# Second output-projection halves ahead of the router transposes, fewer warm-up matmuls, one set of expert weights asked ahead of another

## The chip, the cores and the metric

The kernel runs on one core of a Trainium2 chip. The metric is device time in microseconds (us) for one execution. Five compute engines run their own instruction lists and meet at semaphores: TensorE (PE, matmuls into PSUM banks), VectorE (DVE), ScalarE (ACT), GpSimd (POOL) and SyncE (SP, which here only issues DMAs). Weight loads of TensorE are listed apart as PEld.

## The reference

One layer for 128 context tokens and 512 latent tokens, five tiles of 128 tokens, with a model width of 1024. Cut to what matters here:

```python
x = x + g1 * m                                    # m: mixer output, [y_conv, y_ret] @ w_out
xn = rmsnorm(x, norm_ffn_g) * (1 + sc2) + sh2
x = x + g2 * hier_moe(xn, ...)

# hier_moe
lg_group = t @ w_rg + b_rg                        # 4 groups
gidx = argmax(lg_group)
lg_in = (t @ w_re + b_re) of group gidx           # 8 experts in the group
topv, topi = top_k(lg_in, 2)
w_sel = softmax(topv) * softmax(lg_group)[gidx]
acc = sum over the 2 chosen experts of w_sel * ((silu(t @ w1) * (t @ w3)) @ w2)
```

There are 32 experts of width 256; each has 3 MB of float32 weights: gate (w1), up (w3) and down (w2), 1 MB each. After the layer comes a last norm.

## The kernel before, in words

The order of the work is written out by hand, one instruction list for each engine. The stages: modulation and input projection, convolution and retention, the output projection with the router, and the experts.

**The output projection and the router.** `project(t, half)` multiplies tile t by one half (512 columns) of the output weights, 24 matmuls for tiles 1 to 4 (lines 1138 to 1140, three products of high and low parts for each of eight row blocks), and counts in `wout_mm`. For each half, VectorE's `residual` adds the result to x (`x1_ready`). After both halves `second_norm` writes the tile's normed rows (line 1855, `xn2_ready`), with the sum of squares and the root from ScalarE. `router_T(t)` (line 1359) waits for these rows and transposes them in eight matmuls; ScalarE copies them out of PSUM in two halves (line 1039, `xn2T_ev`); `router(t)` (line 1370) multiplies the copies by the router weights, its first half waiting for the first copy. VectorE's `choose(t)` picks the experts; `ranks(t)` on TensorE (lines 1380 and 1381) counts the tokens before each one; VectorE's `place(t)` writes the slot of each token, and `slots(t)` (line 1390) gathers the slots. For tile t the loop on TensorE runs the projection of tile t beside the router of tile t-1; only for t = 1 do both projection halves come before the transposes.

**From the last tile to the first expert.** On TensorE: `slots`, `ranks(3)`, `clock(14)`, the transposes of tile 4, `clock(2)`, its router, `picked_rows(3)`, `clock_on(5)`, `ranks(4)`, `gathered_rows`, `picked_rows(4)`, `slots(4)`. `clock` and `clock_on` multiply the identity by itself into a bank that is not read (lines 1423 and 1428). `picked_rows` and `gathered_rows` (line 1433) build the rows of the first two experts; the gathered part comes from a DMA that GpSimd issues at line 741 (`first_rows_in`).

**The experts.** Each expert has 64 slots. `gate_up` runs 16 matmuls of 256 columns (lines 1488 and 1492), then VectorE and ScalarE form the hidden values, and `down` (line 1508) multiplies them out.

**The weights of the experts.** Six sets of buffers: `e_slot = (1, 2, 0, 4, 3, 5)`. Some are laid over memory that the output projection uses. `released(sp, slot, FIRST_EXPERT_ITEM)` waits for nine projection halves for slots 0 and 1 (the last tile's first half) and for ten for slots 2 and 3. So set 0 (slot 1) and set 2 (slot 0) are free one projection half before set 1 (slot 2). From the seventh expert on SyncE waits for the gate and up products of the expert that held the slot (`gu_mm`, line 623).

Of the kernel before, what the change touches and what calls it, by code (L numbers as in the profile page):

```python
# [35 lines left out]
FIRST_EXPERT_ITEM = ADA_ALL + N_IN + 2  # L36
# [96 lines left out]
def layer(nc, a, y_prompt, y_sample, new_f, new_b):  # L133
# [8 lines left out]
    with ExitStack() as ctx:  # L142
# [227 lines left out]
        def proj_groups(n):  # L370

            return CB * min(n, 3) + NT * max(n - 3, 0)
# [23 lines left out]
        e_slot = E_SLOTS  # L396
# [59 lines left out]
        def w_down(s, c):  # L456

            if s == RING and c == 0:
                return expert_slot(s)[:, 0:D]
            if s == RING + 1 and c == 1:  # L460
                return arena_b[:, 4352:4352 + D]
            return expert_slot(s)[:, 2 * KT * DE + D * c:2 * KT * DE + D * c + D]
# [20 lines left out]
        def released(eng, slot, item):  # L483

            before = [n for n in range(item) if SLOTS[n] == slot]
            if not before:
                return
            kind, s = items[before[-1]]
            if item == FIRST_EXPERT_ITEM:
                eng.wait_ge(wout_mm, 2 * NT - 1 + (slot in (2, 3)))  # L490
            elif slot == 3 and len(before) == 1:

                eng.wait_ge(proj_mm, proj_groups(N_IN))
            elif kind == "ada":
                eng.wait_ge(mod_mm, s + 1)
            elif kind == "in":

                eng.wait_ge(w_lo_ready, 4 * (s + 1) + 3)
            else:
                eng.wait_ge(wout_mm, 2 * NT - 1 + s)  # L500
# [5 lines left out]
        def _(sp):  # L506
# [11 lines left out]
            def gate_up_weights(s, gate_src, up_src):  # L518
                sp.dma_start(w_gate(s), gate_src).then_inc(ring_in[s], 16)  # L519
                sp.dma_start(w_up(s), up_src).then_inc(ring_in[s], 16)  # L520
# [39 lines left out]
            def gate_up_of(n):  # L560
                gate_up_weights(e_slot[n % NSLOT], gv[n], uv[n])
# [9 lines left out]
            def residual_rows_out(t):  # L571
                sp.wait_ge(x1_ready, 2 * t + 2)
                sp.dma_start(x1_rows[P * t:P * t + P, :], x[:, t, :]).then_inc(x1_out[t // 2], 16)
# [5 lines left out]
            def normed_rows_away(tiles):  # L579
                sp.wait_ge(xs_out[tiles[0] // 2], 16 * len(tiles))  # L580
                sp.wait_ge(xn2T_mm, 2 * tiles[-1] + 2)
# [7 lines left out]
            def down_part_of(n, c):  # L589
                sp.dma_start(w_down(e_slot[n], c), dv[n][:, c, :]).then_inc(down_in[e_slot[n]], 16)  # L590
# [12 lines left out]
            up_of(5)  # L603
            normed_rows_away((2, 3))
            down_part_of(3, 0)
            released(sp, e_slot[1], FIRST_EXPERT_ITEM)
            gate_up_of(1)
            residual_rows_out(NT - 1)
            released(sp, e_slot[2], FIRST_EXPERT_ITEM)
            gate_up_of(2)  # L610

            residual_rows_away((NT - 1,))
            down_part_of(3, 1)
# [476 lines left out]
        def _(pe):  # L1090
# [184 lines left out]
            def late_mod_row(n):  # L1275

                pe.wait_ge(mod_ev, LATE_MODS[n] + 1)
                if n == 0:
                    pe.wait_ge(modrow_ev, len(ROW_MODS))
                    pe.wait_ge(mod_ev, LATE_MODS[0])  # L1280
                    pe.wait_ge(b_late_in, 16 * 2)
                pe.matmul(bank[7 - n][96:98, :], k("sel_rows")[0:SUM_ROWS + 1, 0:2], late_sum[n][0:SUM_ROWS + 1, :],
                          start=True, stop=True).then_inc(modrow_mm, 1)
# [43 lines left out]
            def project(t, half, steps=range(KT)):  # L1327
                n = 2 * t + half
                if t == 0:
                    landed(pe, ADA_ALL + N_IN + half)  # L1330
                if n >= 4 and steps[0] == 0:
                    pe.wait_ge(x1_ready, n - 3)
                if n == 2:
                    pe.wait_ge(mod_ev, ADA_ALL)
                if t == 1:
                    pe.wait_ge(high_act, out_high_done(half, 3))
                    pe.wait_ge(low_dve, (3, 5)[half])
                    pe.wait_ge(low_pool, out_low_done(half))
                if t >= 1 and half == 0:
                    pe.wait_ge(high_act, y_high_done(t, 1))  # L1340
                    pe.wait_ge(low_pool, y_low_done(t))
                w = wide(ADA_ALL + N_IN + half)
                for kt in steps:
                    if t >= 1:
                        low = y_part(t, kt // CB)[1][:, kt % CB, :]
                        last = split_product(bank[n % 4][:, :], (y_hi[(t - 1) % 2][:, kt, :], low),
                                             (out_hi[half][:, kt, :], out_lo[half][:, kt, :]), kt == 0, kt == KT - 1)
                        continue
                    lhs = yconvT[:, kt, P * t:P * t + P] if kt < CB else yretT[:, t, kt - CB, :]
                    last = pe.matmul(bank[n % 4][:, :], lhs, w[:, kt, :], start=(kt == 0), stop=(kt == KT - 1))  # L1350
                if steps[-1] == KT - 1:
                    last.then_inc(wout_mm, 1)

            def router_T(t):
                pe.wait_ge(xn2_ready, t + 1)
                for kt in range(KT):
                    if t >= 1 and kt % 4 == 0:
                        pe.wait_ge(xn2T_ev, 2 * t - 1 + kt // 4)
                    last = pe.transpose(bank[4 + kt // 4][:, P * (kt % 4):P * (kt % 4) + P], xn2[t][:, kt:D:KT], ident)
                    if kt % 4 == 3:  # L1360
                        last.then_inc(xn2T_mm, 1)

            def router(t):
                pe.wait_ge(xn2T_ev, 2 * t + 1)
                if t >= 1:
                    pe.wait_ge(lg_ready, t)
                for kt in range(KT):
                    if kt == HALF_K:
                        pe.wait_ge(xn2T_ev, 2 * t + 2)
                    last = pe.matmul(bank[6][:, 0:GROUPS + EXPERTS], xn2T[:, t % 2, kt, :], w_router[:, kt, :],  # L1370
                                     start=(kt == 0), stop=(kt == KT - 1))
                last.then_inc(rt_mm, 1)

            def ranks(t):

                pe.wait_ge(chosen, t + 1)
                if t >= 1:
                    pe.wait_ge(placed, t)
                both = rt[:, BOTH + EXPERTS * (t % 2):BOTH + EXPERTS * (t % 2) + EXPERTS]
                pe.matmul(bank[7][:, 0:32], k("before"), both, start=True, stop=True)  # L1380
                pe.matmul(bank[7][:, 32:64], k("ones").broadcast_to([P, P]), both, start=True, stop=True).then_inc(rank_mm, 1)
# [13 lines left out]
            for t in range(NT):  # L1395
                project(t, 0)
                if t == 0:
                    late_mod_row(0)
                    late_mod_row(1)
                if t == 1:  # L1400
                    project(t, 1)
                if t >= 1:
                    router_T(t - 1)

                if t == NT - 1:
                    router(t - 1)
                if t == NT - 1:
                    project(t, 1, range(HALF_K + 1))
                    ranks(t - 2)
                    project(t, 1, range(HALF_K + 1, KT))  # L1410
                elif t != 1:
                    project(t, 1)
                if 1 <= t < NT - 1:
                    router(t - 1)
                if t == 3:
                    slots(t - 3)
                if 2 <= t < NT - 1:
                    ranks(t - 2)
            def clock(turns):

                pe.wait_ge(x1_ready, 2 * NT)
                for _ in range(turns):
                    pe.matmul(bank[0][:, 0:P], ident, ident, start=True, stop=True)

            def clock_on(turns):

                for _ in range(turns):
                    pe.matmul(bank[3][:, 0:P], ident, ident, start=True, stop=True)
# [9 lines left out]
            def picked_rows(t):  # L1438

                pe.wait_ge(x1_ready, 2 * NT)  # L1440
                pe.wait_ge(picked, t - NT + 3)
                first_pair(xn2[t], pick[t], t == NT - 2, t == NT - 1)
# [7 lines left out]
            slots(NT - 4)  # L1450
            slots(NT - 3)
            ranks(NT - 2)
            clock(14)
            router_T(NT - 1)
            clock(2)
            router(NT - 1)
            slots(NT - 2)
            picked_rows(NT - 2)
            clock_on(5)
            ranks(NT - 1)  # L1460
            gathered_rows()
            picked_rows(NT - 1)
# [767 lines left out]
```

## Time and profile before

| | us |
|---|---|
| median of 3 runs | 668.73 |
| lowest, highest | 667.97, 671.67 |
| the profiled execution | 670.74 |
| its span, first to last instruction | 669.1 |
| its mean granted TensorE clock | 0.968 |

The page gives the busy share of each engine over the whole span: TensorE 92%, VectorE 48%, GpSimd 24%, ScalarE 23%. These are means over stages with different limits. In the slices of the page the DMA engines are full from about 418 us on, and mostly not full in the stages before; TensorE is full in most slices until about 470 us. Matmul ends are modelled, so that the step from one start to the next says more than the duration of one. A wait for several semaphores is put down to the last of them.

### The profile page before, as it was taken

The numbers are of one execution on the slowest core, as the hardware profiler recorded it, in microseconds if no ns is written. First come the engines' busy times: TensorE is split into PE (matmuls) and PEld (weight loads), VectorE is DVE, ScalarE is ACT, GpSimd is POOL, SyncE is SP. The second block draws the span as 40 slices with busy tenths as digits, with TensorE's granted clock in tenths as the row PEclk, the third lists the DMA queues.
The fourth block names the chain that finished last, engine by engine and source line by source line (L and its number), as shares of the span: only waits on it lengthen the run. The fifth ranks groups of instructions, "written<-read, shape, count | busy, mean of one in ns | idle before, by whom it ended". The sixth has DMA issues, their size and how long they took to land.

```text
span 669.1 us, 9054 instructions
## 1 busy us (share of the span) xinstructions
PE 612.7 (92%) x3712; PEld 437.3 (65%) x3712; DVE 318.4 (48%) x631; ACT 154.1 (23%) x297; POOL 160.4 (24%) x124
## 2 busy tenths in 40 slices
PE   3799999999999989999699899999998788889796
PEld 3579999988888865744588797555554444445342
DVE  1433118706240445718768763455454555334326
ACT  5325432122312233354221111101101000001014
POOL 0042724333242200027330011222221111111110
PEclk9989999999999999999799889999999888899999
DMA  7985240320303269788552798999999999999977
GB/s 278 387 295 219 70 153 1 126 89 37 126 0 126 69 227 394 255 317 323 190 196 89 292 390 331 414 418 418 420 417 417 418 420 417 421 417 418 416 279 299
DMA packets 50381, 183.83 MB, mean 275 GB/s; under 512 B 5861, under 2 KB 6037, under 8 KB 38945
## 3 DMA queue, kind: packets, MB, share of 16 engines
q1 hardware_dynamic: 42156, 161.59, 61.9%
q0 software_dynamic: 7216, 18.99, 7.9%
q10 hardware_dynamic: 964, 2.63, 1.1%
q8 instruction: 31, 0.51, 0.3%
q14 instruction: 14, 0.11, 0.0%
HBM read 172.79 MB, written 16.81 MB: 283 GB/s over the span
## 4 chain that ended last, share of the span: by engine, by line
PE 66%; DMA 20%; DVE 7%; SPq 4%; ACT 2%; issue 1%; DVEq 0%; POOLq 0%; ACTq 0%
PE bank L1138 12%; PE bank L1139 11%; PE bank L1140 11%; PE bank L1488 9%; DMA ring<-in_w_up_e 8%; DMA arena_ab<-in_w_up_e 4%; DMA x<-in_w_up_e 4%; PE bank L1508 4%; PE bank L1097 3%; DMA ring<-expert_out_rows 2%; PE bank L1433 2%; PE bank L1114 2%; DVE out_lo L480 1%; SPq L519 1%; PE bank L1192 1%
## 5 line engine op out<-in xcount | busy, mean ns | idle before, releaser
L1488 PE MATMUL bank<-ring,arena_ab 128*64 128x256 f32 x352 | 83.3, 392 | 10.1 <-DMA ring<-in_w_up_e 9.6
L680 POOL TENSOR_TENSOR w_lo<-ring,w_hi 128x1024 fp32r<-128x1024 f32 x25 | 61.4, 2458 | 112.5 <-ACT w_hi L864 112.5
L1492 PE MATMUL bank<-ring,arena_ab 128*64 128x256 f32 x352 | 83.3, 392 | 0.0
L1488 PEld LDWEIGHTS bank<-ring,arena_ab 128*64 128x64 f32 x352 | 48.9, 141 | 46.8 <-DMA ring<-in_w_up_e 17.5
L1622 DVE TENSOR_TENSOR arena_ab<-arena_ab,bank 64x256 f32<-64x256 f32 x32 | 19.5, 610 | 113.3 <-ACT arena_ab L1045 113.3
L1138 PE MATMUL bank<-arena_ab_r,w_hi 128*128 128x320 f32 x192 | 62.2, 324 | 3.0 <-DVE xn_lo L1622 2.9
L786 POOL DMA_INDIRECT expert_out_rows<-arena_ab,row_out x32 | 32.0, 1001 | 130.9 <-DVE arena_ab L1622 130.9
L1138 PE MATMUL bank<-w_hi,arena_ab_r 128*128 128x512 f32 x160 | 63.3, 396 | 0.0
L1139 PE MATMUL bank<-w_lo,arena_ab_r 128*128 128x512 f32 x160 | 62.9, 393 | 0.0
L1140 PE MATMUL bank<-w_hi,xn_lo 128*128 128x512 f32 x160 | 62.8, 393 | 0.0
L1139 PE MATMUL bank<-xn_lo,w_hi 128*128 128x320 f32 x192 | 59.9, 312 | 0.0
L1140 PE MATMUL bank<-arena_ab_r,w_lo 128*128 128x320 f32 x192 | 59.8, 311 | 0.0
L1045 ACT ACTIVATE arena_ab<-bank 64x256 f32<-64x256 f32 x32 | 12.0, 376 | 205.0 <-PE bank L1492 205.0
L864 ACT ACTIVATE w_hi<-ring 128x1024 fp32r<-128x1024 f32 x25 | 26.5, 1062 | 114.1 <-PE bank L1140 114.1
L1492 PEld LDWEIGHTS bank<-ring,arena_ab 128*64 128x64 f32 x352 | 48.9, 141 | 0.0
L1508 PE MATMUL bank<-ring,arena_ab 128*64 128x512 f32 x176 | 42.6, 605 | 0.9 <-ACT arena_ab L1049 0.9
L1138 PEld LDWEIGHTS bank<-arena_ab_r,w_hi 128*128 128x128 f32 x192 | 36.9, 192 | 6.1 <-issue 5.0
L1140 PEld LDWEIGHTS bank<-arena_ab_r,w_lo 128*128 128x128 f32 x192 | 37.0, 193 | 0.0
L1139 PEld LDWEIGHTS bank<-xn_lo,w_hi 128*128 128x128 f32 x192 | 37.0, 193 | 0.0
L1140 PEld LDWEIGHTS bank<-w_hi,xn_lo 128*128 128x128 f32 x160 | 30.0, 188 | 7.2
L1139 PEld LDWEIGHTS bank<-w_lo,arena_ab_r 128*128 128x128 f32 x160 | 30.1, 188 | 6.7
L1138 PEld LDWEIGHTS bank<-w_hi,arena_ab_r 128*128 128x128 f32 x160 | 30.1, 188 | 6.6
(289 smaller groups left out, 1123.1 us busy)
## 6 DMA issues: line engine op xcount, KB each, us to landing
ring<-in_w_ada SPq DMA_DIRECT2D x11, 2048.0 KB, 12.3
ring<-in_w_down_e SPq DMA_DIRECT2D x22, 1024.0 KB, 25.8
ring<-in_w_gate_e SPq DMA_DIRECT2D x22, 1024.0 KB, 23.1
ring<-in_w_up_e SPq DMA_DIRECT2D x22, 1024.0 KB, 26.0
ring<-in_w_in SPq DMA_DIRECT2D x6, 2048.0 KB, 8.4
arena_ab<-in_w_down_e SPq DMA_DIRECT2D x15, 512.0 KB, 24.0
x<-in_w_gate_e SPq DMA_DIRECT2D x5, 1024.0 KB, 25.8
arena_ab<-in_w_gate_e SPq DMA_DIRECT2D x5, 1024.0 KB, 24.0
```

Source lines behind the costliest of these rows:

```text
L680: pool.tensor_tensor(as_piece(w_lo[p_ % 2], p_), piece_of(w, p_), as_piece(w_hi[p_ % 2], p_), ALU.subtract).then_inc(w_lo_ready, 1)
L786: pool.indirect_dma_start(half_rows, bass.IndirectOffsetOnAxis(ap=column, axis=0), ysb[:, p_, :], None, bounds_check=2 * 2 * TOK - 1, oob_ ...
L864: act.activation(as_piece(w_hi[piece % 2], piece), piece_of(w, piece), ACT.Copy).then_inc(w_hi_ready, 1)
L1097: last = pe.matmul(out[32 * j:32 * j + 32, :], cs[:, kt, :], w[:, kt, :], start=(kt < 4), stop=(kt >= 4))
L1114: last = pe.matmul(bank[4 + 2 * (t % 2) + half][:, P * c:P * c + P], x[:, t, P * kt:P * kt + P], diag[:, t, :], start=True, stop=True)
L1138: pe.matmul(out, lhs[0], rhs[0], start=start, stop=False)
L1139: pe.matmul(out, lhs[0], rhs[1], start=False, stop=False)
L1140: return pe.matmul(out, lhs[1], rhs[0], start=False, stop=stop)
L1488: pe.matmul(bank[2 + p_][0:BLK, 0:DE], lhs, w_gate(s)[:, kt, :], start=(kt == 0), stop=(kt == KT - 1))
L1492: last = pe.matmul(bank[2 + p_][BLK:2 * BLK, 0:DE], lhs, w_up(s)[:, kt, :], start=(kt == 0), stop=(kt == KT - 1))
L1508: last = pe.matmul(bank[6 + p_][BLK * half:BLK * half + BLK, :], hidT[:, p_, c, :], w_down(s, c)[:, SL * half:SL * half + SL], start=(c == ...
L1622: return dve.tensor_tensor(out, in0, in1, op)
```

## The change

Three edits, all of order or count. On TensorE, the second projection halves of tiles 2 and 3 come before the transposes of the tile in front, as that of tile 1 does already. The warm-up matmuls after `ranks(3)` are 5 and not 14, those before `ranks(4)` 2 and not 5. On SyncE, the gate and up weights of set 2 are asked for before those of set 1, and the residual rows of the last tile are sent out after both.

```diff
@@ SyncE
             down_part_of(3, 0)
+            released(sp, e_slot[2], FIRST_EXPERT_ITEM)
+            gate_up_of(2)
             released(sp, e_slot[1], FIRST_EXPERT_ITEM)
             gate_up_of(1)
             residual_rows_out(NT - 1)
-            released(sp, e_slot[2], FIRST_EXPERT_ITEM)
-            gate_up_of(2)
@@ TensorE
-                if t == 1:
+                if t in (1, 2, 3):
                     project(t, 1)
                 if t >= 1:
                     router_T(t - 1)
...
-                elif t != 1:
+                elif t not in (1, 2, 3):
                     project(t, 1)
                 if 1 <= t < NT - 1:
                     router(t - 1)
...
             ranks(NT - 2)
-            clock(14)
+            clock(5)
             router_T(NT - 1)
...
             picked_rows(NT - 2)
-            clock_on(5)
+            clock_on(2)
             ranks(NT - 1)
```

On TensorE, in the turn of tile 2, this is the place between the two projection halves (the high and low parts of the first half's weights are out_hi_53 and out_lo_55, those of the second half out_hi_54 and out_lo_56; line 1359 is the transposes of tile 1):

```order
 L1139 MATMUL bank<-out_lo_55,arena_cd_r 128x512
 L1140 MATMUL bank<-out_hi_53,arena_ab_r 128x512
-L1359 MATMUL bank<-kept,arena_ab 128x128 x8
 L1138 MATMUL bank<-out_hi_54,arena_cd_r 128x512
 L1139 MATMUL bank<-out_lo_56,arena_cd_r 128x512
```

The eight transposes leave this place, and the two halves follow each other. On TensorE, 24 matmuls later in the same turn, this is the end of the second half (line 1370 is the router of tile 1, line 1380 the ranks of tile 0):

```order
 L1139 MATMUL bank<-out_lo_56,arena_cd_r 128x512
 L1140 MATMUL bank<-out_hi_54,arena_ab_r 128x512
+L1359 MATMUL bank<-kept,arena_ab 128x128 x8
 L1370 MATMUL bank<-w_router,arena_ab 128x36 x8
 L1380 MATMUL bank<-arena_cd,kept 128x32
```

Transposes and router of one tile now stand side by side; the turn of tile 3 reads the same. On SyncE, after the last projection's first half, the requests stand like this (line 519 asks for gate weights, line 520 for up weights, line 573 sends residual rows out):

```order
 L519 DMA ring<-in_w_gate_e 128x2048
 L520 DMA ring<-in_w_up_e 128x2048
-L573 DMA residual_rows<-x 128x1024
 L519 DMA ring<-in_w_gate_e 128x2048
 L520 DMA ring<-in_w_up_e 128x2048
+L573 DMA residual_rows<-x 128x1024
 L590 DMA arena_ab<-in_w_down_e 128x1024
```

The residual rows move behind both pairs; which set a pair belongs to does not show in the rows, but the first pair is now set 2 and the second set 1. The lists of VectorE, ScalarE and GpSimd are the same in both kernels.

## Rows read from the trace of the kernel before

**Rows 1.** Windows: us, busy by engine, PEclk, DMA share, GB/s.

```profile
380.00:382.00 2.00, 1.06 (x5) 0.53 (x3) 1.89 (x8) 0.00 (x0) 0.88 (x1) 1.00 0.14 57
406.00:408.00 2.00, 1.56 (x21) 1.24 (x21) 1.45 (x7) 1.81 (x2) 0.19 (x1) 1.00 0.59 119
480.00:630.00 150.00, 129.11 (x876) 69.04 (x874) 70.76 (x125) 12.42 (x38) 26.57 (x28) 0.94 1.02 418
```

**Rows 2.** Timeline of SyncE: start, us, line, operation; the requests for weights.

```profile
369.78 0.33 SPq L519 DMA_DIRECT2D ring<-in_w_gate_e  x1
...
381.09 0.33 SPq L519 DMA_DIRECT2D ring<-in_w_gate_e  x1
...
383.25 0.45 SPq L519 DMA_DIRECT2D ring<-in_w_gate_e  x1
...
394.78 0.33 SPq L519 DMA_DIRECT2D ring<-in_w_gate_e  x1
...
410.37 0.33 SPq L519 DMA_DIRECT2D ring<-in_w_gate_e  x1
```

**Rows 3.** Chain that ended last, from 383 us: start, us, what.

```profile
383.37 4.83 PE bank L1423 x28
...
395.83 2.00 PE bank L1428 x10
...
398.19 7.71 PE bank L1433 x32
...
406.67 0.40 PE bank L1488
```

**Rows 4.** Timeline of TensorE, tile 3's transposes and router [idle before <-releaser].

```profile
369.59 1.04 PE L1359 MATMUL bank<-kept,arena_ab 128*128 128x128 f32 x8
371.45 1.95 PE L1370 MATMUL bank<-w_router,arena_ab 128*128 128x36 f32 x16 [0.83 <-ACT arena_ab L1039]
```

**Rows 5.** Timeline of VectorE, last tile's residual, normed rows and choice.

```profile
369.78 0.69 DVE L1622 TENSOR_TENSOR arena_cd<-bank,arena_ab 128x512 f32<-128x512 f32 x1 [1.71 <-PE bank L1140]
...
384.90 1.28 DVE L1855 SCALAR_TENSOR_TENSOR arena_ab<-arena_ab,stat 128x1024 f32<-128x1024 f32 x1
...
394.72 0.92 DVE L1622 TENSOR_TENSOR arena_cd<-arena_cd 128x8 f32<-128x8 f32 x5
```

**Rows 6.** Timeline of TensorE, transposes and routers of tiles 0 and 1.

```profile
331.67 1.04 PE L1359 MATMUL bank<-kept,arena_ab 128*128 128x128 f32 x8
332.96 1.97 PE L1370 MATMUL bank<-w_router,arena_ab 128*128 128x36 f32 x16 [0.25 <-ACT arena_ab L1039]
334.77 0.48 PE L1138 MATMUL bank<-out_hi,arena_cd_r 128*128 128x512 f32 x1
...
340.46 1.06 PE L1359 MATMUL bank<-kept,arena_ab 128*128 128x128 f32 x8
341.28 0.48 PE L1138 MATMUL bank<-out_hi,arena_cd_r 128*128 128x512 f32 x1
...
346.97 1.87 PE L1370 MATMUL bank<-w_router,arena_ab 128*128 128x36 f32 x16
348.68 0.39 PE L1380 MATMUL bank<-arena_cd,kept 128*128 128x32 f32 x2
```

**Rows 7.** Timeline of GpSimd, the first gather's issue.

```profile
385.73 1.41 POOL L741 DMA_INDIRECT arena_cd<-expert_in_rows,idx  x1 [3.66 <-DVE idx L1841]
```

**Rows 8.** DMA issues over the span: count, KB, median us to landing.

```profile
ring<-in_w_up_e SPq DMA_DIRECT2D x22, 1024.0 KB, 26.0
...
arena_cd<-expert_in_rows,idx POOLq DMA_INDIRECT x16, 8.5
```

**Rows 9.** Windows around the routers of tiles 0 and 3, PEclk third from the end.

```profile
332.70:336.11 3.41, 3.16 (x23) 2.92 (x23) 2.08 (x4) 2.97 (x7) 2.11 (x2) 1.00 0.38 154
...
370.24:373.66 3.42, 2.59 (x22) 2.39 (x21) 3.00 (x15) 1.08 (x2) 0.00 (x0) 1.00 0.86 275
373.66:377.07 3.41, 3.41 (x10) 2.66 (x9) 2.89 (x18) 0.00 (x0) 0.00 (x0) 0.50 1.02 428
```

## The prediction

> **What bounds the kernel now.** I read the windows first, stage by stage, since the average over the span hides that there are two limits. From 480 to 630 us the DMA engines are full at 418 GB/s and TensorE waits inside the expert loop [rows 1]: there the load stream is the bound. Before that, around 380 us, the lanes moved 57 GB/s, and at 406 to 408 us 119 GB/s [rows 1], so they had room. The second view is SyncE's own issue list. After the first six sets of weights are asked for, nothing more can be asked until the first expert's gate and up products free a slot: that issue stands at 410.37 us [rows 2], 3.7 us after the first expert's first matmul at 406.67 us [rows 3]. So the full stream that ends the kernel hangs on the start of the first expert, and what moves that start moves the end by as much. What moves only a load that lands before its use moves nothing.
>
> What sets 406.67 us is the third view, the chain of waits from 363 us on. It runs on TensorE through the last projection's first half (its end is the router transpose's start, 369.59 us [rows 4]), crosses to VectorE at 369.78 us, where that engine had idled 1.71 us for the bank [rows 5], and stays with VectorE until the normed rows of the last tile are written at 384.90 + 1.28 = 386.18 us [rows 5]. Then it is TensorE's again: warm-up matmuls until 388.20 us, router, picked rows, warm-up, ranks, gathered rows at 398.19 us, first expert [rows 3].
>
> **The change, part by part.**
>
> *Second halves ahead of the router transposes, tiles 2 and 3.* No instruction is added or taken away. Before, the transposes of tile 1 took 340.46 to 341.28 us = 0.82 us, and the router matmuls, a projection half later, 346.97 to 348.68 us = 1.71 us, with no wait at either: 2.53 us [rows 6]. The half product between them covered ScalarE's copy of the transposed rows. After the change the router follows the transposes at once, as it does for tile 0 already. There the pair took 331.67 to 334.77 us = 3.10 us, with an idle of 0.25 us put down to ScalarE [rows 6]. So each of the two places costs 3.10 - 2.53 = 0.57 us, and nothing covers it, since TensorE is the engine that VectorE waits for at 369.78 us. Bounds: 0.25 us each by the idle alone, 0.83 us each by the largest such idle, at 371.45 us [rows 6, 4]; I take 0.57, the whole pair measured. What is won is that each second half ends 0.82 us sooner, so that VectorE gets its second residual and norm sooner; but VectorE already idles before 369.78 us, so this is worth nothing. ScalarE's high part of tile 4 now waits behind the copy of tile 1 and not the other way round; only the last projection uses it, a whole tile later, so it costs nothing. Sum of this part: +1.1 us on the whole chain from 369.78 us.
>
> *Warm-up 14 to 5.* The fourteen took 4.83 us, 0.345 us each, and ended at 388.20 us [rows 3], 2.0 us after the rows that the next transposes wait for. With 0.1 us for the hand-over, 1.9 us of them were too long. Five take 1.7 us, from 383.37 + 1.1 = 384.5 to 386.2 us, and the rows come at 386.18 + 1.1 = 387.3 us. So the wait for the rows takes the place of the matmuls, and the part gives back 1.9 us; TensorE idles 1.1 us instead.
>
> *Warm-up 5 to 2.* Five took 2.00 us [rows 3], 0.40 us each. VectorE's choice, for which the ranks wait behind them, was ready at 394.72 + 0.92 = 395.64 us [rows 5], when these matmuls began (395.83 us). All five are on the path, three fewer give back 1.2 us. Were each as short as half of that, as at the clock's upper level, 0.6 us.
>
> *Third set asked ahead of the second.* The slot of the third set is free one projection half sooner, so its two requests move from 383.25 us to just after the group that begins at 369.78 us; the second set's keep their place at about 381.09 us [rows 2], and the last residual rows go out behind both. 2 MB at 418 GB/s are 5.0 us of the lanes, of which part falls into the empty stretch at 380 us. The second set is asked for 25 us before the first expert even begins, the third is used after the second; both land long before. Residual rows, the remaining down parts and the fifth set follow a few us later, all used after 410 us. Worth nothing at the end by itself.
>
> The gather of the first rows could be touched: it is issued at 385.73 us and SyncE is released by it at 394.78 us, 9.05 us later [rows 2, 7]. Moved by +1.1 us it lands at 395.9 us, and the gathered rows would begin at 398.19 - 2.0 = 396.2 us: covered, with 0.3 us to spare. What it would cost if the deeper queue held it back: bounds nothing and the whole 5.0 us of the third set's transfer. I take nothing, since in the full stream such gathers land in 8.5 us while the weights asked on SyncE's queue take 26.0 us [rows 8], so a gather does not stand behind them.
> The Trainium skill, DMA: Bandwidth & Descriptors, section on queues, rings and completion order, says that each DMA engine goes round the queues that have work, packet by packet; by that rule the depth of the other queue adds nothing, which is the value taken, and the landings of the full stream agree with it [rows 8].
>
> Sum: +1.1 - 1.9 - 1.2 = -2.0 us at the first expert, and as much at the end. The profiled execution took 670.74 us (a span of 669.1 and 1.6 around it), so 668.7 us; against the median of the runs shown, 668.73 us, it is 666.7 us.
>
> **The rivals.**
>
> *The router stretches pull the clock down.* From 369.59 to 371.45 + 1.95 = 373.40 us TensorE did only transposes and router, with 0.83 us idle; the granted clock was 1.0 in 370.24 to 373.66 us and 0.50, which is 1.2 of 2.4 GHz, in the 3.41 us after [rows 4, 9]. The projection in that stretch ran at half speed: 3.41/2 = 1.7 us lost. There it cost nothing, as VectorE was late anyway. The change makes two more such stretches, of 3.1 us and the ranks behind, on the path. Against it: around the same pair of tile 0 the granted clock stayed at 1.00 from 332.70 to 336.11 us [rows 9]. It decides from both places on: -2.0 + 3.4 = +1.4 us, slower, 670.1 us. With one place it is -0.3 us, 668.4 us.
> The Trainium skill, TensorE: Matmul & The Clock Gate, section on HAM oscillation, puts the fall down to idle gaps longer than any of these. By the page the sum stays -2.0 us; the row at 373.66 us shows a fall behind 0.83 us of idle, and the measurement decides, so the rival keeps its chance.
>
> *Less warm-up, and the first expert starts at half speed.* The same rows bear it out in kind: little work, then 0.50. The gathered and picked rows lie between (7.71 us [rows 3]), which speaks against. A half-speed stretch of 3.41 us in the first expert costs 1.7 us and so holds its slot that much longer: -0.3 us, 668.4 us.
>
> *The gather comes late.* 1 us late gives -1.3 us, 667.4 us; all 5.0 us behind the new transfer gives 400.9 instead of 396.2 us, +2.7 us, 671.4 us.
>
> *The lanes are the bound already from 370 us.* Then filling the empty stretch, up to 1.7 us of 380 to 382 us, comes on top: -3.7 us, 665.0 us. Against it stand the 119 GB/s at 406 us.
>
> *The warm-up is not what the path waits for:* the rows come later than I think, only +1.1 - 1.2 remains, 668.6 us.
>
> **How the numbers follow.** Forecast, 666.7 us: 0.45. Clock after the router stretches: 0.16, a quarter of it with both places. Clock at the first expert: 0.18. Late gather: 0.10. Lanes as the bound: 0.06. Warm-up not on the path: 0.05. The order's bounds (0.5 to 1.7 us for both places) and the second warm-up's (0.6 to 1.2) make the forecast's own range 666.1 to 667.9 us. The runs shown go from 667.97 to 671.67 us, so I put about 1.5 us on either side of the cases: 664.6 to 670.4 us. Half a per cent is 3.3 us, about what can be told from no change. Below 665.4 us lie most of the lanes' case and a tail of the forecast, 0.12; above 672.1 us only the worst gather and the worst clock with a bad run, 0.03; 0.85 between.
>
> **What would show it.** Right: a router start some 0.5 us behind the transposes' end for tiles 1 and 2; the last projection's first half ending about 1.1 us later; an idle of about 1 us before the last tile's transposes, put down to VectorE, and these starting 0.8 us sooner; gathered rows and first expert 2.0 us sooner; the step from first expert to end unchanged. Wrong: a clock of 0.50 in the projection of tiles 3 or 4 or in the first expert; gathered rows that wait for a DMA; a first slot release at 408.4 us without an earlier end.

## The result and the profile after

The changed kernel takes 672.76 us (median of 20 runs, 670.20 to 675.93), the kernel before 669.46 us (median of 20 runs measured with it): a ratio of 1.0046, 95% interval 1.0034 to 1.0057, which is +3.1 us (2.3 to 3.8). The forecast was 666.7 us, within 664.6 to 670.4 us. It was wrong in sign and outside its range. The profiled execution of the changed kernel took 673.58 us, its span is 671.9 us (669.1 before), its mean granted clock 0.964.

All work up to the first router is the same code, yet that router starts at 331.57 us here and at 332.96 us in the profile before. Tile 1's second half, just ahead of that router, ran at 0.50 until 326.4 us here and until 329.3 us before. So I count every stage from the first router's start; the table gives the distance and what each stage adds. "Last" means of tile 4.

| stage begins, us behind the first router | before | after | added in the stage before it |
|---|---|---|---|
| tile 3's transposes | 36.62 | 39.25 | +2.63 |
| last transposes | 55.08 | 55.68 | -2.03 |
| picked rows (line 1433) | 58.67 | 62.24 | +2.97 |
| last ranks | 64.70 | 66.80 | -1.47 |
| first expert | 73.71 | 75.81 | 0.00 |
| last expert's last down product | 305.25 | 307.75 | +0.40 |
| end of the span | 336.15 | 340.37 | +1.72 |

The five stages to the first expert add 2.10 us, all 4.22 us; less the 1.39 us by which the first router came sooner, this is the 2.8 us between the spans.

TensorE's timeline of the changed kernel (start us, us, line, operation, [idle before <-releaser]):

```profile
344.67 1.05 PE L1359 MATMUL bank<-kept,arena_ab 128*128 128x128 f32 x8
345.96 1.98 PE L1370 MATMUL bank<-w_router,arena_ab 128*128 128x36 f32 x16 [0.24 <-ACT arena_ab L1039]
...
359.52 1.05 PE L1359 MATMUL bank<-kept,arena_ab 128*128 128x128 f32 x8
360.87 1.98 PE L1370 MATMUL bank<-w_router,arena_ab 128*128 128x36 f32 x16 [0.30 <-ACT arena_ab L1039]
...
370.82 1.04 PE L1359 MATMUL bank<-kept,arena_ab 128*128 128x128 f32 x8
372.69 1.95 PE L1370 MATMUL bank<-w_router,arena_ab 128*128 128x36 f32 x16 [0.83 <-ACT arena_ab L1039]
...
382.60 0.65 PE L1390 MATMUL bank<-b_ada_rows,modsum 128*64 128x16 f32 x16 [1.83 <-DVE b_ada_rows L1926]
...
383.92 2.10 PE L1423 MATMUL bank<-kept 128*128 128x128 f32 x10
387.25 1.97 PE L1359 MATMUL bank<-kept,arena_ab 128*128 128x128 f32 x8 [1.23 <-DVE arena_ab L1855]
389.02 1.06 PE L1423 MATMUL bank<-kept 128*128 128x128 f32 x4
389.87 3.46 PE L1370 MATMUL bank<-w_router,arena_ab 128*128 128x36 f32 x16
...
393.81 4.19 PE L1433 MATMUL bank<-arena_ab 128*128 128x128 f32 x16
397.80 0.73 PE L1428 MATMUL bank<-kept 128*128 128x128 f32 x4
...
398.73 4.05 PE L1433 MATMUL bank<-kept,arena_cd 128*128 128x128 f32 x16
...
407.38 0.40 PE L1488 MATMUL bank<-ring,arena_ab 128*64 128x256 f32 x1 [0.44 <-ACT arena_ab L1056]
```

The routers of tiles 1 and 2 now follow their transposes with the idle for ScalarE's copy, 0.24 and 0.30 us, that tile 0 had [rows 6]. Before the last transposes TensorE idles 1.23 us for VectorE's normed rows, as the forecast said. What it did not say stands in the next rows: eight transposes take 1.97 us and the router 3.46 us. In the kernel before:

```profile
382.16 0.65 PE L1390 MATMUL bank<-b_ada_rows,modsum 128*64 128x16 f32 x16 [1.10 <-DVE b_ada_rows L1926]
...
388.04 1.05 PE L1359 MATMUL bank<-kept,arena_ab 128*128 128x128 f32 x8
...
389.39 1.97 PE L1370 MATMUL bank<-w_router,arena_ab 128*128 128x36 f32 x16
...
391.63 4.19 PE L1433 MATMUL bank<-arena_ab 128*128 128x128 f32 x16
```

The transposes and the router, the same instructions, took 1.05 and 1.97 us there. The picked rows take 4.19 us in both. The gather of the slots (line 1390) is taken up under the order below. The windows of the changed kernel say why (us, busy by engine, PEclk third from the end, DMA share, GB/s):

```profile
380.00:382.00 2.00, 0.77 (x4) 0.29 (x2) 1.76 (x11) 0.00 (x0) 0.95 (x1) 1.00 1.03 328
406.00:408.00 2.00, 1.56 (x17) 1.29 (x18) 0.94 (x6) 1.34 (x2) 0.00 (x0) 1.00 0.74 262
480.00:630.00 150.00, 128.56 (x872) 68.64 (x870) 69.91 (x125) 12.39 (x38) 27.18 (x27) 0.94 1.02 418
363.92:367.33 3.41, 3.41 (x10) 2.63 (x9) 2.19 (x11) 0.00 (x0) 0.55 (x1) 0.50 0.37 154
384.40:387.81 3.41, 2.18 (x12) 1.89 (x11) 3.20 (x11) 0.85 (x3) 1.06 (x1) 0.50 1.01 425
387.81:391.22 3.41, 3.41 (x18) 3.41 (x17) 1.81 (x10) 2.48 (x3) 0.92 (x2) 0.50 1.02 423
391.22:394.64 3.42, 3.42 (x21) 3.31 (x22) 1.09 (x7) 0.00 (x0) 0.00 (x0) 0.50 0.98 391
394.64:398.05 3.41, 3.41 (x17) 3.41 (x16) 2.52 (x15) 0.32 (x2) 0.00 (x0) 0.50 0.48 136
```

And the same stretch of the kernel before:

```profile
383.90:387.31 3.41, 3.41 (x18) 3.41 (x18) 3.15 (x13) 0.34 (x3) 1.57 (x2) 0.50 0.99 346
387.31:390.72 3.41, 3.41 (x32) 3.36 (x32) 1.35 (x8) 1.97 (x3) 0.41 (x1) 1.00 0.95 368
...
394.14:397.55 3.41, 3.41 (x17) 3.41 (x16) 1.29 (x8) 0.32 (x2) 0.00 (x0) 0.50 1.01 418
397.55:400.96 3.41, 3.41 (x19) 3.41 (x18) 2.45 (x15) 0.00 (x0) 0.00 (x0) 1.00 1.03 416
```

The granted clock fell to 0.50 at about 384 us in both, after TensorE had been busy in part only (0.77 of 2.00 us from 380 to 382 us, 1.06 before [rows 1]). Before, the fourteen warm-ups filled that stretch (3.41 of 3.41 us busy) and the clock was 1.00 again when the transposes came. After, five leave TensorE busy for 2.18 of 3.41 us, and the clock stays at 0.50 until 398 us. Busy time alone does not settle it: from 387.81 to 398.05 us transposes, router and picked rows keep TensorE busy in every stretch, and the clock stays down. The kernel before has a fall of its own there, from 394.14 to 397.55 us, under the picked rows and the five warm-ups before the last ranks. The other new stretch of 0.50 is the projection behind tile 2's router, 363.92 to 367.33 us. The load stream is what it was, 418 GB/s from 480 to 630 us [rows 1].

VectorE's timeline of the changed kernel, with its last wait for loaded rows of expert results:

```profile
371.02 0.69 DVE L1622 TENSOR_TENSOR arena_cd<-bank,arena_ab 128x512 f32<-128x512 f32 x1 [4.71 <-PE bank L1140]
...
385.91 1.28 DVE L1855 SCALAR_TENSOR_TENSOR arena_ab<-arena_ab,stat 128x1024 f32<-128x1024 f32 x1
...
661.87 0.69 DVE L1622 TENSOR_TENSOR ring<-ring 128x512 f32<-128x512 f32 x1 [1.71 <-DMA ring<-expert_out_rows]
```

That last row in the kernel before:

```profile
659.02 0.69 DVE L1622 TENSOR_TENSOR ring<-ring 128x512 f32<-128x512 f32 x1 [0.39 <-DMA ring<-expert_out_rows]
```

At 371.02 us VectorE had idled 4.71 us for the bank, not 1.71 us [rows 5]: the path there is TensorE's, with no slack. At the end it waits 1.71 us, not 0.39 us, for the last load. The DMA queues from 654 to 662 us (queue: packets, MB, share), after:

```profile
q1 hardware_dynamic: 857, 3.24, 101.2%
q8 instruction: 1, 0.02, 0.8%
```

One 16 KB packet of the instruction queue, program code, lies among the last loads. Before, the same window holds only `q1`; the last code fetch came at 643 us, 26 us before the end, and here 13 us before it. The change takes away 24 TensorE matmuls with their weight loads, 48 instructions, and with them the code stands elsewhere.

### The profile page after: what moved, and what is told of

The parts are those of the page before. It is cut to its first block, busy times and chain, and to the rows that moved or that the text cites. A ratio compares the mean times of both kernels' runs of the same rounds, so it can differ in the third digit from the quotient of the medians.

```text
span 671.9 us, 9006 instructions
## 1 busy us (share of the span) xinstructions
PE 609.9 (91%) x3688; PEld 433.6 (65%) x3688; DVE 316.5 (47%) x631; ACT 153.8 (23%) x297; POOL 160.2 (24%) x124
## 3 DMA queue, kind: packets, MB, share of 16 engines
q10 hardware_dynamic: 964, 2.63, 1.1%
## 4 chain that ended last, share of the span: by engine, by line
PE 66%; DMA 21%; DVE 7%; ACT 2%; issue 2%; SPq 2%; DVEq 0%; POOLq 0%; ACTq 0%
PE bank L1138 12%; PE bank L1139 11%; PE bank L1140 11%; PE bank L1488 10%; DMA ring<-in_w_up_e 8%; DMA arena_ab<-in_w_up_e 4%; DMA x<-in_w_up_e 4%; PE bank L1508 4%; PE bank L1097 3%; DMA ring<-expert_out_rows 2%; PE bank L1433 2%; PE bank L1114 2%; DMA expert_out_rows<-arena_ab,row_out 2%; PE bank L1370 1%; PE bank L1480 1%
```

## Experiments

All runs are timed beside the kernel before, whose median was 669.69 to 669.75 us; microseconds of a ratio are its distance from 1 times that. Distances in the text are again from the first router. The end stretch is the time from the last expert's last down product to the end, 30.90 us before and 32.62 us after.

**One edit at a time.** The order on TensorE alone:

```diff
-                if t == 1:
+                if t in (1, 2, 3):
                     project(t, 1)
...
-                elif t != 1:
+                elif t not in (1, 2, 3):
```

> Only the order of the second projection halves changes. Clock theory (the turns of tiles 2 and 3 cost 0.5 us each uncovered, and the projection after one of them runs at half clock for 3.4 us, as in the trace of the changed kernel at 363.9 us): +1.1 to +2.8 us against the kernel before. Prediction's own step: +1.1 us. Rival, loads (the request order makes the loss): +1 us at most here. A half-clock stretch in the projection of tile 3 or 4 in the profile speaks for the first.

670.85 us, ratio 1.0020 (1.0006 to 1.0033): +1.3 us. Tile 3's transposes come at 37.72 us, +1.10 us where 1.1 us was forecast, and the end stretch is 30.66 us. There is no fall behind tile 2's router in this profile, and none behind tile 3's, where the kernel before has one [rows 9]. Two rows of TensorE:

```profile
381.75 0.65 PE L1390 MATMUL bank<-b_ada_rows,modsum 128*64 128x16 f32 x16 [1.86 <-DVE b_ada_rows L1926]
...
405.86 0.40 PE L1488 MATMUL bank<-ring,arena_ab 128*64 128x256 f32 x1 [0.44 <-ACT arena_ab L1056]
```

The gather of the slots comes 11.81 us behind tile 3's transposes here, and 12.57 us before. The first expert comes at 73.64 us, 0.07 us sooner than before. So in this execution, the fastest of the twelve (669.90 us), nothing of the 1.10 us is left at the first expert; the loss of 1.3 us is shown by the times, not by a profile.

Both warm-ups alone:

```diff
-            clock(14)
+            clock(5)
...
-            clock_on(5)
+            clock_on(2)
```

> Only the two warm-up counts change (14 to 5, 5 to 2). Prediction's own step: -3.1 us. Clock theory: the rows are waited for with an idle of about 1.2 us, the clock falls to 0.50, the last tile's transposes and router take 5.2 us and not 2.5; -3.1 + 2.8 = -0.3 us at the first expert. Rival, loads: -3 us. The granted clock between 384 and 398 us and the durations of the transposes and the router decide.

669.81 us, ratio 1.0007 (0.9993 to 1.0021): no change where -3.1 us was forecast. The last transposes and router in its profile:

```profile
386.59 1.97 PE L1359 MATMUL bank<-kept,arena_ab 128*128 128x128 f32 x8 [1.14 <-DVE arena_ab L1855]
...
389.21 3.47 PE L1370 MATMUL bank<-w_router,arena_ab 128*128 128x36 f32 x16
```

The transposes start 1.78 us sooner, at 53.30 us, and end later. The end stretch is 32.21 us. This profiled execution (672.16 us) was the slowest of the twelve: the five executions with a mean granted clock of at most 0.967 took 671.5 us on average, the other seven 669.2 us, so the long stretch at 0.50 may not come in each; that is judged from the mean clock alone.

SyncE's requests alone:

```diff
+            released(sp, e_slot[2], FIRST_EXPERT_ITEM)
+            gate_up_of(2)
             released(sp, e_slot[1], FIRST_EXPERT_ITEM)
             gate_up_of(1)
             residual_rows_out(NT - 1)
-            released(sp, e_slot[2], FIRST_EXPERT_ITEM)
-            gate_up_of(2)
```

> Only the third set is asked ahead of the second. Clock theory and prediction: no change, within 0.7 us. Rival, loads: the residual rows land some 4 us later (395.6 against 390.9 us in the two profiles), everything asked behind them is late, and the end is +2 to +3 us.

669.68 us, ratio 0.9998 (0.9982 to 1.0014): nothing.

The first warm-up alone, `clock(14)` to `clock(5)`:

> Only the first warm-up is shortened, 14 to 5; the second stays at 5. Prediction's own step: -1.9 us. Clock theory: the long half-clock stretch comes from the idle behind the first warm-up, so the transposes and the router take 2.8 us longer here too, and the sum is -1.9 + 2.8 = +0.9 us, slower than with nothing changed. If the second warm-up were what kept the clock up, the transposes and router would stay at 2.5 us and the time would be -1.9 us.

670.84 us, ratio 1.0021 (1.0007 to 1.0035): +1.4 us, a loss. The profile repeats the 1.97 and 3.47 us of the run above. Its first expert comes 0.56 us later than before, where 1.9 us sooner was forecast, and its end stretch is 1.2 us longer (32.08 us), so that the loss is not the clock's alone. By the times the second warm-up is worth about -0.9 us (0.5 less 1.4, with intervals that overlap), and the first is what turned over.

**The place of the code.** The changed kernel, with the 48 instructions put back as tiny matmuls (a matmul and a weight load each) where TensorE waits for weights anyway:

```diff
+                if n in (24, 26):
+                    for _ in range(6):
+                        pe.matmul(bank[2 + p_][0:32, 0:16], ident[:, 0:32], ident[:, 0:16], start=True, stop=True)
```

> The changed kernel with 12 tiny matmuls (32 weights, 16 columns, into a bank that the next products overwrite) in the expert loop before experts 24 and 26, where TensorE waits for weights anyway; they put back the instructions that the shorter warm-ups took out. Code-fetch theory (with fewer instructions, TensorE's last 16 KB of code is fetched at 658.9 us, among the loads of the expert results, and not at 643 us before them; the engine that fetches finishes its share about 1 us late): the fetch goes back ahead of those loads, the last load is waited for 0.4 us and not 1.7, and the time is 1.3 us below the changed kernel, +1.8 us above the kernel before. Rival, clock alone: no difference from the changed kernel (+3.1 us).

670.42 us, ratio 1.0013 (1.0001 to 1.0026): 2.2 us better than the changed kernel (1.0034 to 1.0057) with more work in it; above the kernel before it is 0.9 us, where 1.8 us was expected. The last code fetch is back at 25.9 us before the end, the end stretch at 31.24 us. That is 1.4 us by the profile; the rest is less clear, since this profile also has no fall behind tile 2's router and a shorter one at the last transposes.

The opposite test, the kernel before with nothing but 52 such matmuls:

```diff
+                if n in (20, 22, 24, 26):
+                    for _ in range(13):
+                        pe.matmul(bank[2 + p_][0:32, 0:16], ident[:, 0:32], ident[:, 0:16], start=True, stop=True)
```

> The kernel before with 52 tiny matmuls (32x16) in front of experts 20, 22, 24 and 26, where TensorE waits for weights anyway: nothing but the place of the code changes. Theory A (an instruction fetch among the last loads delays them): the last 16 KB fetch falls 10 to 17 us before the end instead of 26 us, VectorE waits 1.3 to 1.7 us for the last loaded rows instead of 0.39 us, the stretch from the last down products to the end takes 32.0 to 32.6 us instead of 30.9 us, and the time is +1.3 us, ratio 1.002. Theory B (the fetch is beside the point, the longer tail of the changed kernel has to do with its router stages): the fetch moves but the stretch keeps 30.9 us and the ratio is 1.000.

670.54 us, ratio 1.0011 (0.9997 to 1.0025). VectorE's last wait and the DMA queues from 654 to 662 us in its profile (two views):

```profile
658.75 0.69 DVE L1625 TENSOR_TENSOR ring<-ring 128x512 f32<-128x512 f32 x1 [1.64 <-DMA ring<-expert_out_rows]
```

```profile
q1 hardware_dynamic: 586, 2.14, 66.4%
q8 instruction: 1, 0.02, 1.0%
```

The fetch is at 12.8 us before the end, the wait 1.64 us, the end stretch 32.15 us: each as in the changed kernel, with the routers untouched. The other two profiles with the warm-ups cut and no pads (both, and the first alone) have their last fetch 13 to 14 us before the end too, and waits of 1.65 and 1.57 us. The profile settles where the 1.3 us of the end come from; the time alone (+0.7 us, interval just over zero) would not.

**Warm-up where the clock falls.** Before tile 1's second projection half TensorE idles 5.75 us for split weights, and that half then begins at 0.50 in every profile so far. Twenty identity matmuls ahead of tile 1's first half move that first half into the idle:

```diff
+                if t == 0:
+                    for _ in range(20):
+                        pe.matmul(bank[3][:, 0:P], ident, ident, start=True, stop=True)
```

> The kernel before, with 20 identity matmuls in TensorE's idle ahead of tile 1's projection. Clock theory: the projection then runs at 1.00 and not 0.50 in its first stretch, TensorE reaches the router of tile 0 up to 3.4 us sooner, and since TensorE bounds the chain there, the first expert and the end come 2 to 3.4 us sooner. Rival (VectorE or the low parts bound that stage): 0 to -0.5 us.

671.32 us, ratio 1.0022 (1.0010 to 1.0035): slower, where 2 to 3.4 us less was expected, although the first expert starts at 403.69 instead of 406.67 us. TensorE's timeline behind the last expert:

```profile
638.58 2.94 PE L1594 MATMUL bank<-kept 128*128 128x128 f32 x24 [3.24 <-issue]
```

It idles 3.24 us with no engine that released it, and 16 KB code fetches run at 636.0 and 639.3 us; that it waits for its own instructions is inferred from the two. In the kernel before, this step follows the last expert at once. The end stretch is 33.19 us, so 2.3 of the 3.0 us went there. The profiled execution (669.59 us) is among the fastest of the twelve; why the median lies 1.7 us above it no profile shows. More instructions do not bring this wait each time: the run with 52 tiny matmuls, 208 instructions, has none at this place.

Warm-ups 9 and 2 in the kernel before, with the code's place kept by eight tiny matmuls as above:

```diff
-            clock(14)
+            clock(9)
...
-            clock_on(5)
+            clock_on(2)
```

> The kernel before with the first warm-up at 9 and the second at 2, the instructions put back by 8 tiny matmuls in the expert loop. Clock theory (it is the idle behind the first warm-up that lets the clock fall, and the fall doubles the last transposes and router): with 9 there is little idle, the transposes and router stay at 2.5 to 3.5 us, and the cut is worth what the prediction gave it, -1.5 - 1.2 = -2 to -2.7 us. If the clock falls for another reason: +0.5 us as with 5 and 2.

668.14 us, ratio 0.9978 (0.9965 to 0.9991): -1.5 us. The last transposes in its profile:

```profile
386.73 1.35 PE L1359 MATMUL bank<-kept,arena_ab 128*128 128x128 f32 x8
...
388.39 1.98 PE L1370 MATMUL bank<-w_router,arena_ab 128*128 128x36 f32 x16
```

No idle ahead, the router at full speed, the first expert 2.7 us sooner (71.00 instead of 73.71 us; with five and two it was 73.65 us). This was the warm-ups' real surplus: five of fourteen, not nine.

The changed kernel with the twenty matmuls and the pads together:

> The changed kernel with both additions: 20 identity matmuls ahead of tile 1's projection, 12 tiny ones in the expert loop. If the three terms add up: +3.1 - 1.3 - 3 = about -1 us against the kernel before. If the order of the router is hurt more by the clock (both router stretches at 0.50): up to +2 us.

673.08 us, ratio 1.0051 (1.0038 to 1.0064): +3.4 us, above either forecast. The wait behind the last expert is 3.02 us here. Its profiled execution, 669.42 us, was the fastest of six (the others 672.4 to 674.0 us), so why the rest is slower no profile shows.

Both good pieces without moving the code: eight wide matmuls in place of twenty small ones, and warm-ups 9 and 2 (eight in, eight out):

```diff
+                if t == 0:
+                    for _ in range(8):
+                        pe.matmul(bank[3][:, 0:384], ident, kept[:, 0:384], start=True, stop=True)
...
-            clock(14)
+            clock(9)
...
-            clock_on(5)
+            clock_on(2)
```

> The kernel before with two edits: eight warm-up matmuls of 384 columns in TensorE's idle before tile 1's projection, and warm-ups 9 and 2 instead of 14 and 5 (eight in, twelve out, of four instructions each at most: the instruction count hardly moves). Theory A (places add up where the code keeps its place): the run with warm-ups 9 and 2 gave -1.5 us and a first expert 2.7 us after R0 sooner; the run with twenty small warm-ups had its first expert 3.0 us sooner and lost that in the tail to late code. With wide matmuls in place of many small ones the code keeps its place, so both gains reach the end: first expert near 401 to 402 us instead of 406.7 us, stretch from last expert's down products to the end 30.7 to 31.3 us, time -4 to -5 us, ratio 0.993. Theory B (the gain at the first expert doesn't reach the end, the lanes bound it): no better than -1.5 us, ratio 0.998, and the step from first expert to last down products grows by some 3 us from 231.5 us.

664.75 us (7 runs), ratio 0.9943 (0.9922 to 0.9964): the best version here, 4.9 us by the medians, 3.8 us (2.4 to 5.2) by the ratio. TensorE's timeline:

```profile
322.86 0.47 PE L1138 MATMUL bank<-out_hi,arena_ab_r 128*128 128x512 f32 x1 [0.79 <-issue]
...
400.78 0.40 PE L1491 MATMUL bank<-ring,arena_ab 128*64 128x256 f32 x1 [0.44 <-ACT arena_ab L1056]
```

The idle of 5.75 us is 0.79 us, the first expert starts 5.9 us sooner, and from there to the last down product it takes 231.52 us as before (231.54 us). What the first expert gains does reach the end; this step of the forecast holds.

**The order and the clock.** The changed kernel with nine instead of five warm-ups and eight pads:

```diff
-            clock(5)
+            clock(9)
```

> The changed kernel with nine warm-ups instead of five ahead of the last transposes (two in the second place stay), and eight tiny matmuls that keep the code's place at the end. Theory A (five warm-ups were too few: TensorE idled 1.2 us, the clock stayed at 0.50 through the last transposes and router; nine leave no such idle): clock 1.00 in the last transposes and router, their 16 transposes and router matmuls in 3.3 to 3.6 us instead of 6.0 us, and the time -1.2 us against the kernel before (+1.1 order, -2.3 warm-up), ratio 0.998; +0.5 us, ratio 1.001, should a profile show 0.50 behind tile 2's router. Theory B (it is the order that makes the clock fall at the last transposes, whatever the warm-up): 0.50 again and +1 us or more, ratio 1.0015 or above.

669.55 us, ratio 1.0000 (0.9985 to 1.0016): the whole loss of the changed kernel is gone, though not below the kernel before. The pads alone had taken off 2.2 us; the further 0.9 us of the nine warm-ups lie within intervals that overlap. From the last transposes to the picked rows it takes 3.59 us again, not 6.56 us. Windows of its profile:

```profile
364.10:367.50 3.40, 3.40 (x9) 2.63 (x8) 1.99 (x11) 0.00 (x0) 0.55 (x1) 0.50 0.37 154
...
405.00:408.40 3.40, 3.27 (x16) 2.16 (x18) 1.22 (x6) 1.28 (x1) 1.82 (x2) 0.50 1.01 429
```

The fall behind tile 2's router is there again (tile 3's transposes at 39.22 us), and another at the start of the first expert, whose stretch to the last down product is 232.38 us, 0.84 us longer.

The two orders together, with the warm-ups of before (the first and third diff of this section):

> The changed kernel with its warm-ups put back to 14 and 5: the order on TensorE and the order of SyncE's requests together. The parts alone gave +1.3, +0.5 and -0.1 us (order, both warm-ups, requests), 1.7 us in all, and the changed kernel +3.1 us. Theory A (the parts add; what is over comes from order and warm-ups together, behind the same routers): +1.2 us, ratio 1.002, and the last transposes and router 3.6 us from the transposes' start to the picked rows, as with fourteen warm-ups before. Theory B (the two orders together make the clock fall behind tile 2's router, as in two of the three profiles that hold both with the same code up to there): +2.5 us or more, ratio 1.004, with 0.50 around 364 to 367 us and the last transposes' predecessor 39.2 us behind the first router instead of 37.7 us.

671.48 us, ratio 1.0038 (1.0021 to 1.0055): +2.5 us. Windows behind tile 2's router:

```profile
360.30:363.70 3.40, 3.10 (x31) 2.96 (x31) 3.01 (x5) 2.00 (x5) 0.00 (x0) 1.00 0.38 154
363.70:367.10 3.40, 3.40 (x10) 2.66 (x9) 2.16 (x11) 0.00 (x0) 0.55 (x1) 0.50 0.37 154
```

The same stretches with the order on TensorE alone:

```profile
361.00:364.40 3.40, 3.10 (x31) 2.84 (x31) 2.98 (x6) 2.19 (x5) 0.00 (x0) 1.00 0.38 154
364.40:367.80 3.40, 3.40 (x15) 2.74 (x15) 2.37 (x11) 0.00 (x0) 0.55 (x1) 1.00 0.37 154
```

The work is alike, the clock is not. That the swap of the requests makes the difference can't be: it acts first at 372.8 us, behind this place. So the same list of TensorE's instructions falls to 0.50 here in some executions and not in others: in three profiles (changed kernel, the run with nine warm-ups, this one), and not in two (order alone, pads; the one with twenty matmuls ahead left aside). In the three the first router starts at 331.35 to 331.57 us, in the two at 332.22 and 332.59 us. The intervals of this run and of the order alone overlap. What decides it is open.

## Why the prediction was wrong

**Warm-up 14 to 5: the step that failed.** "So the wait for the rows takes the place of the matmuls, and the part gives back 1.9 us; TensorE idles 1.1 us instead." The idle came as said (1.23 us), and the transposes started sooner: by 1.78 us in the run of this edit alone; of the 2.03 us in the table 0.5 us stand in the run with both orders and fourteen warm-ups too. But the idle was priced at nothing. The fourteen, most of them at 0.50, kept TensorE busy until the clock came back, 3.4 us after it had fallen. With five, transposes and router ran at half speed, +2.97 us. Alone the part cost +1.4 us (0.5 to 2.3), by its profile 0.56 us at the first expert and 1.2 us in the end stretch. With nine in the kernel before, and the code's place kept, it took 3.91 us from the transposes to the picked rows (6.56 us in the changed kernel) and the first expert came 2.7 us sooner. The rival "less warm-up" looked for the half speed at the first expert, some 20 us too far on; the step from the last ranks to the first expert is the same 9.01 us in both profiles, because the clock is at 1.00 again from 398 us on in both.

The Trainium skill, TensorE: Matmul & The Clock Gate, section on HAM oscillation, ties the fall to long idle gaps. By that alone gaps of about a microsecond would cost nothing. Here a clock that was already at 0.50 stayed there for 13.65 us in the three profiles with five warm-ups and gaps of 1.05 to 1.23 us (changed kernel, both warm-ups, the first alone), and for 6.83 us in the two with gaps of 0.82 and 0.83 us (the runs with pads, without and with the twenty matmuls); it came back after 3.4 us in the runs with nine warm-ups and no gap. That the gap alone decides this is not shown.

**Order: the term was right where it was read, +1.1 us at tile 3's transposes** (1.10 us by the profile of the order alone). At the end only the times show it, 1.3 us (0.4 to 2.2). Its rival, the clock behind the router, came true at one of the two places in three of five profiles, for a further 1.5 us (2.63 less 1.10). And one reading of the rival was wrong: the fall behind tile 3's router in the kernel before did not cost nothing. From tile 3's transposes to the gather of the slots it takes 12.57 to 12.61 us in the eight profiles with that fall, and 11.78 to 11.81 us in the six without, whichever the order (11.80 us in the run with twenty matmuls, without the fall and with the old order; 12.60 us in the changed kernel with nine warm-ups, with it). Five of the six profiles with the changed order are without it, which gives back 0.8 us.

**Warm-up 5 to 2: the right way, its size between the forecast's two bounds.** By the times it is -0.9 us, where 1.2 us was forecast and 0.6 us was the bound for the upper level. The table's -1.47 us holds more than three matmuls: before, the five ran at 0.50 (2.00 us, [rows 3]); with only the first warm-up cut they run partly at 1.00, and dropping three of them brings the last ranks 0.61 us forward.

**Requests: right**, nothing. SyncE's requests in the changed kernel:

```profile
371.02 0.33 SPq L519 DMA_DIRECT2D ring<-in_w_gate_e  x1
...
373.03 0.43 SPq L519 DMA_DIRECT2D ring<-in_w_gate_e  x1
...
396.95 0.47 SPq L519 DMA_DIRECT2D ring<-in_w_gate_e  x1
...
411.08 0.33 SPq L519 DMA_DIRECT2D ring<-in_w_gate_e  x1
```

The third set's requests moved to 373.03 us from 383.25 us, just behind the group of 371.02 us, and the first request for a released slot comes at 411.08 us, 3.7 us behind the first expert as before [rows 2, 3]. The gathered rows, at 398.73 us, did not wait for their gather. The lanes' empty stretch at 380 to 382 us did fill, 328 GB/s for 57, and at 406 to 408 us they moved 262 GB/s for 119 [rows 1], still short of full: neither moved the end.

**"And as much at the end": not quite.** From the first expert on, the table has 0.40 + 1.72 us more. Of the 1.72 us, 1.3 us are the last loads behind a code fetch, a cost that no part of the forecast had: it counted which matmuls go and not that the program gets shorter. The Trainium skill, Runtime: NRT & Kernel Launch, section on instruction fetch mechanics, says that engines refill their instruction memory in 16 KB blocks and that the cost of crossing a block is mostly hidden. The traces show the 16 KB packets. Hidden they are not at the end, where 1.3 us of VectorE's waiting (1.71 less 0.39) hang on one. The other 0.4 us of the end stretch are not traced.

**The sum.** Forecast +1.1 - 1.9 - 1.2 = -2.0 us. Shown in the profiles: tile 3's transposes +1.1 and in some executions +1.5; first warm-up and what the order gives back -2.0, half speed +3.0; second -1.5; the run through the experts +0.4, the end +1.7: +4.2 us. The times of the parts add up as well: order and requests together +2.5 us (1.4 to 3.7), both warm-ups alone +0.5 us (-0.5 to 1.4), 3.0 of the 3.1 us. So the warm-ups missed their -3.1 us by 3.6 us and the order its +1.1 us by 1.4 us. The +0.4 us is not traced to one cause; the granted clock was 0.50 from 623.3 to 626.7 us, among the last experts.

## What to carry to other kernels

Before a warm-up is cut, read the granted clock of the stretch that it fills and of the work behind it: a warm-up at 0.50 with work at 1.00 behind it is buying that, and only what outlasts the wait behind it may go, with no idle left. Where the clock is already at 0.50, an idle on TensorE just ahead of a chain of small matmuls is priced with that chain at half speed, as here. And an edit that adds or removes instructions can move later code fetches, here one into the last loads, so compare variants of a few microseconds with the instruction count held equal, by wide matmuls or by pads in a stage that waits anyway.

## What the runs showed of the hardware

- Half the clock doubles some instructions and leaves others: eight transposes 1.05 to 1.97 us, sixteen router matmuls 1.97 to 3.46 us, the sixteen picked-row matmuls take 4.08 to 4.10 us at 1.00 (three runs with nine warm-ups) and 4.19 us at 0.50.
- One 16 KB code fetch among full-rate loads took 1.03 us on its DMA engine and lengthened the wait for the last of these loads by 1.3 us, to 1.71 us; with the fetch elsewhere it was 0.38 to 0.44 us.
- Behind the last expert TensorE stood 3.24 and 3.02 us, released by no engine, in the two runs with 80 more instructions ahead of that place; that it waited for code is inferred.
- The same instructions on TensorE get 1.00 in one execution and 0.50 in another, 364 us into the program, with the start of the first router 0.65 to 1.24 us apart.
- TensorE can be busy throughout and stay at 0.50: 387.81 to 398.05 us in the changed kernel, with transposes, router and picked rows.
